# Weight groups of the KC chunk loaded between the stripes of x, the 112-column product moved into the VS chunk, and the last chunk finished per token tile

## What is computed

```python
u = RMSNorm(h)
[q | k/v x3 | nsa gates | z | xBC | dt | branch gates] = u @ W_in
A = NSA(q, ...)        # compressed + selected + sliding-window attention, a sigmoid gate per head
B = Mamba2-SSD(z, xBC, dt)
h = h + W_out( sigmoid(gA) * (A @ P_A) + sigmoid(gB) * (B @ P_B) )
h = h + relu(RMSNorm(h) @ W_up)^2 @ W_down
out = RMSNorm(h)
```

## Time and profile before

| | |
|---|---|
| median of 3 runs | 2117.24 us (2115.2 to 2118.54) |
| the profiled execution | 2118.04 us |
| its span, first to last instruction | 2116.4 us |
| mean granted clock of TensorE | 0.997 |
| TensorE busy | 2083.1 us, 98% of the span |
| VectorE busy | 1310.9 us, 62% |
| ScalarE busy | 977.1 us, 46% |
| GpSimd busy | 112.3 us, 5% |
| bytes moved | 383.59 MB, mean 181 GB/s |

### The profile page before, as it was taken

One profiled execution on the slowest core, in us unless ns is written; L12 is line 12 of the kernel. 1 busy time (PEld: TensorE's weight loads), 2 busy tenths in 40 slices (PEclk: granted clock), 3 DMA queues, 4 the chain that ended last, 5 costly groups with the idle time before them and its releaser, 6 DMA issues.

```text
span 2116.4 us, 28060 instructions
## 1 busy us (share of the span) xinstructions
PE 2083.1 (98%) x9760; PEld 1731.3 (82%) x9760; DVE 1310.9 (62%) x1780; ACT 977.1 (46%) x1323; POOL 112.3 (5%) x162
## 2 busy tenths in 40 slices
PE   7999999999999999999999999999999999999997
PEld 5788888888888888888888878888888888888886
DVE  5645666666665578886678865555555555555554
ACT  5434444444443455554455534444434434433443
POOL 3000000000000011111011100000000000000000
PEclk9999999999999999999999999999999999999999
DMA  8556464645466666665656556556566566666653
GB/s 234 186 166 188 140 179 139 177 138 174 138 197 195 175 179 188 181 184 195 188 170 183 183 197 207 179 183 189 190 195 184 188 194 184 188 195 193 184 191 133
DMA packets 196631, 383.59 MB, mean 181 GB/s; under 512 B 16192, under 2 KB 16288, under 8 KB 195120
## 3 DMA queue, kind: packets, MB, share of 16 engines
q1 hardware_dynamic: 193152, 365.87, 57.1%
q0 software_dynamic: 3344, 16.24, 2.2%
q10 hardware_dynamic: 32, 0.01, 0.0%
HBM read 379.91 MB, written 2.16 MB: 181 GB/s over the span
## 4 chain that ended last, share of the span: by engine, by line
PE 59%; issue 36%; DVE 2%; DMA 1%; ACT 1%; DVEq 0%; ACTq 0%; SPq 0%; POOLq 0%; POOL 0%
PE acc L284 17%; PE acc L286 17%; PE acc L285 17%; PE x L802 1%; PE tr L307 1%; DMA raw<-w_in 1%; PE x L738 1%; PE x L687 1%; PE tr L760 1%; DVE lo L251 1%; PE x L745 0%; PE tr L762 0%; PE tr L753 0%; PE tr L765 0%; PE x L814 0%
## 5 line engine op out<-in xcount | busy, mean ns | idle before, releaser
L251 DVE TENSOR_TENSOR lo<-raw,hi 128x1024 fp32r<-128x1024 f32 (+1 forms) x696 | 847.0, 1224 | 591.3 <-ACT hi L244 581.0
L244 ACT ACTIVATE hi<-raw 128x1024 fp32r<-128x1024 f32 (+1 forms) x696 | 724.5, 1052 | 699.6 <-PE acc L286 676.4
L284 PE MATMUL acc<-hi,LAh 128*128 128x512 f32 x1856 | 738.0, 398 | 4.0 <-DVE lo L251 4.0
L286 PE MATMUL acc<-hi,LAl 128*128 128x512 f32 x1856 | 724.1, 390 | 0.0
L285 PE MATMUL acc<-lo,LAh 128*128 128x512 f32 x1856 | 723.0, 390 | 0.0
L284 PEld LDWEIGHTS acc<-hi,LAh 128*128 128x128 f32 x1856 | 348.7, 188 | 78.0 <-issue 3.9
L286 PEld LDWEIGHTS acc<-hi,LAl 128*128 128x128 f32 x1856 | 348.4, 188 | 73.6
L285 PEld LDWEIGHTS acc<-lo,LAh 128*128 128x128 f32 x1856 | 348.8, 188 | 72.2 <-issue 1.7
L284 PE MATMUL acc<-hi,LBh 128*128 128x512 f32 x896 | 352.6, 394 | 2.7 <-DVE LBl L339 2.7
L286 PE MATMUL acc<-hi,LBl 128*128 128x512 f32 x896 | 350.0, 391 | 0.0
L285 PE MATMUL acc<-lo,LBh 128*128 128x512 f32 x896 | 349.8, 390 | 0.0
(11 more groups left out here) (267 smaller groups left out, 1174.1 us busy)
## 6 DMA issues: line engine op xcount, KB each, us to landing
raw<-w_in SPq DMA_DIRECT2D x304, 512.0 KB, 4.0
raw<-w_up SPq DMA_DIRECT2D x128, 512.0 KB, 3.9
raw<-w_down SPq DMA_DIRECT2D x128, 512.0 KB, 4.4
raw<-w_proj_ssm SPq DMA_DIRECT2D x64, 512.0 KB, 4.0
raw<-w_proj_nsa SPq DMA_DIRECT2D x32, 512.0 KB, 4.4
raw<-w_out SPq DMA_DIRECT2D x32, 512.0 KB, 4.4
W<-acs_rows POOLq DMA_DIRECT2D x8, 1024.0 KB, 5.0
GA<-x SPq DMA_DIRECT2D x4, 512.0 KB, 5.9
```

The lines of the kernel that those rows point to most:

```text
L244: act.activation(hi[:, sl, :, 0:n], raw[:, sl, :, 0:n], ACT.Copy).then_inc(s_hi, 1)
L251: dve.tensor_tensor(lo[:, sl, :, 0:n], raw[:, sl, :, 0:n], hi[:, sl, :, 0:n].bitcast(F32), ALU.subtract).then_inc(s_lo, 1)
L284: pe.matmul(o, xh, wh, start=(k == 0), stop=False)
L286: x = pe.matmul(o, xl, wh, start=False, stop=(k == KT - 1))
```

## The change

- The chunk `C_SMALL` is gone; every later chunk has a number lower by one. Its weights are loaded by GpSimd in two transfers (48 and 64 columns, all 2048 rows) once the first `compress` is done, split by ScalarE and VectorE in one piece each (`small_hi`, `small_lo`), and multiplied in four parts after groups 3 to 6 of the VS chunk. `gates_dt`, `softplus` and `cumsums` move to the KW chunk, the last turn and copies to the VW chunk.
- SP issues the weight groups of the KC chunk between the stripes of x. TensorE multiplies group 0 after two of the four stripes; the turns of the other two are hooks after groups 0 and 3.
- `angles` and `reduce_angles` move to slots 3 and 4 of the VC chunk, `sines` to slot 5, `columns` to slot 1. The squares of x move to slots 3 and 4 of the KC chunk.
- The counts of `s_lo` for the quarters of `w1` become 8n + 2q + 4.
- ScalarE runs a one-column copy before it needs its table for x.
- At the end TensorE does groups 6 and 7 of the last chunk first for token tile 0 and then for tile 1; adding, weighing, squares, variance and inverse root run per tile; the four stores wait for a piece each, and the last is issued by ScalarE.

```diff
-            for n in range(4):
+            def load_x(n):
                 sp.dma_start(GA[:, :, NC * n:NC * (n + 1)], x_rows[:, :, NC * n:NC * (n + 1)]).then_inc(s_x[n], 16)
+            load_x(0)
+            load_group(sp, C_KC, 0, w_in, 0, KC0)
+            load_group(sp, C_KC, 1, w_in, 0, KC0)
+            load_x(1)
+            load_group(sp, C_KC, 2, w_in, 0, KC0)
+            load_x(2)
+            load_group(sp, C_KC, 3, w_in, 0, KC0)
+            load_group(sp, C_KC, 4, w_in, 0, KC0)
+            load_x(3)
+            for j in (5, 6, 7):
+                load_group(sp, C_KC, j, w_in, 0, KC0)
-            load_chunk(sp, C_SMALL, w_in, 0, 0, extra=[(w_in, NG0, 0, 3 * NH), (w_in, DT0, 3 * NH, SH)])
...
-                    pool.wait_ge(s_lo, 8 * n + 2 * q + 6)
+                    pool.wait_ge(s_lo, 8 * n + 2 * q + 4)
...
+            pool.wait_ge(s_hid, 1)
+            pool.dma_start(SMG, w_in[:, :, NG0:NG0 + 3 * NH]).then_inc(s_smw, 16)
+            pool.dma_start(SMD, w_in[:, :, DT0:DT0 + SH]).then_inc(s_smw, 16)
...
+            turn_x(0)
+            turn_x(1)
+            mm_chunk(pe, C_KC, 0, LAh, LAl, {0: [lambda: turn_x(2)], 3: [lambda: turn_x(3)]},
+                     need={0: [(s_trd, 1)], 2: [(s_trd, 2)], 4: [(s_trd, 3)], 6: [(s_trd, 4)]})
+            mm_chunk(pe, C_VC, 1, LAh, LAl, {0: [turn_columns], 2: [lambda: pe_turn(pe, E_KC, XR, [(s_acc, C_KC + 1)])],
+                                             6: [lambda: compress(0)]})
+            mm_chunk(pe, C_KS, 0, LAh, LAl, {0: [compress_k2],
...
+            mm_chunk(pe, C_VS, 1, LAh, LAl, {0: [compress_v2],
+                                             2: [lambda: pe_turn(pe, E_KS, Y, [(s_rope, 1)])],
+                                             3: [lambda: small(0)], 4: [lambda: small(1)], 5: [lambda: small(2)],
+                                             6: [lambda: small(3)]})
+            mm_chunk(pe, C_KW, 0, LAh, LAl, {0: [turn_small], 6: [cumsum]})
...
+            slots(act, split_hi, C_KC, 8, {2: [lambda: split_x(3)], 3: [lambda: squares_of_x(0)], 4: [lambda: squares_of_x(1)],
+                                           7: [take_kc]})
+            slots(act, split_hi, C_VC, 8, {2: [lambda: copy_t(E_KC, KV[:, 0:2, :])], 5: [sines], 6: [lambda: hidden(0, 1)],
+                                           7: [lambda: take(C_VC, 1, XR[:, 0, :])]})
...
+            slots(dve, split_lo, C_KC, 8, {2: [lambda: split_x(3)], 7: [take_kc]})
+            slots(dve, split_lo, C_VC, 8, {1: [columns], 2: [lambda: blocks(0, E_KC, CPK)], 3: [angles, lambda: reduce_angles(0)],
+                                           4: [lambda: reduce_angles(1)], 6: [lambda: hidden(0)],
+                                           7: [lambda: take(C_VC, 1, XR[:, 1, :], C_VC + 1)]})
...
+            for t, done, v in ((0, s_l0, 1), (1, s_mm, 8 * C_END)):
+                dve.wait_ge(done, v)
+                dve.tensor_tensor(H[:, t, c3], acc[(C_END - 1) % 2][t][:, :], H[:, t, c3], ALU.add).then_inc(s_la, 1)
+                dve.drain()
+                dve.tensor_tensor(GB[:, t, c3], H[:, t, c3], GA[:, 0, c3], ALU.mult).then_inc(s_hw, 1)
+                last_variance(t)
+            for t, n in ((0, 1), (1, 0)):
+                dve.wait_ge(s_fr, t + 1)
+                dve.tensor_scalar(GB[:, t, HALF[n]], GB[:, t, HALF[n]], RS[:, t:t + 1], None, ALU.mult).then_inc(s_fin[t][n], 1)
```

More of the change, by code:

```diff
@@ L72 @@
 C_MLP = C_WO + 4
+C_END = C_MLP + 32
 C_END = C_MLP + 32
@@ L287, in mm_group, with mm_rows @@
             x.then_inc(s_mm, 1)
+        def mm_rows(pe, g, par, j, t, Lh, Ll):
+            sl = g % RING
+            pe.wait_ge(s_lo, g + 1)
+            for kk in range(2):
+                k = 2 * j + kk
+                o, xh, xl = acc[par][t][:, :], Lh[:, k, t * P:(t + 1) * P], Ll[:, k, t * P:(t + 1) * P]
+                pe.matmul(o, xh, hi[:, sl, kk, :], start=False, stop=False)
+                pe.matmul(o, xh, lo[:, sl, kk, :], start=False, stop=False)
+                x = pe.matmul(o, xl, hi[:, sl, kk, :], start=False, stop=(k == KT - 1))
+            return x
         def pe_event(pe, e, ready=()):
@@ L940, in hidden @@
                 act.activation(HT[:, :], X7[:, 0:NG * NCMP], ACT.Tanh, scale=0.5).then_inc(s_hta, 1)
-            slots(act, split_hi, C_SMALL, 8, {0: [lambda: squares_of_x(0)], 1: [lambda: squares_of_x(1)], 7: [copy_small]})
-            slots(act, split_hi, C_KC, 8, {1: [gates_dt], 2: [softplus], 6: [sines], 7: [lambda: take(C_KC, 1, XR[:, 0, :])]})
-            slots(act, split_hi, C_VC, 8, {0: [decay_ends, copy_cumsums], 2: [lambda: copy_t(E_KC, KV[:, 0:2, :])], 6: [lambda: hidden(0, 1)],
-                                           7: [lambda: take(C_VC, 0, XR[:, 0, :])]})
@@ new lines, in _ @@
+            slots(act, split_hi, C_VS, 8, {0: [small_hi], 2: [lambda: copy_t(E_KS, key_cols(0, 0))],
+                                           7: [lambda: take(C_VS, 1, V_(0, 0)), copy_small]})
+            slots(act, split_hi, C_KW, 8, {1: [gates_dt], 2: [softplus], 7: [lambda: take(C_KW, 0, XR[:, 0, :])]})
+            slots(act, split_hi, C_VW, 8, {0: [decay_ends, copy_cumsums], 2: [lambda: copy_t(E_KW, key_cols(1, 0))],
+                                           7: [lambda: take(C_VW, 1, V_(0, 1))]})
@@ L1099, in mlp @@
                     hk[8 * k + 10] = [lambda k=k: act_split_t(act, e + k, LAh, 4 * k)]
-                    if last:
+                    if last and k < 3:
                         hk[8 * k + 39] = [lambda k=k: residual_squares(C + 4 + k, k)]
@@ L1276, in take_rope, with small_lo @@
                 rope()
-            slots(dve, split_lo, C_SMALL, 8, {})
-            slots(dve, split_lo, C_KC, 8, {1: [gates_dt], 2: [columns, angles], 3: [softplus],
-                                           4: [lambda: reduce_angles(0)], 5: [lambda: reduce_angles(1)], 6: [cumsums], 7: [lambda: take(C_KC, 1, XR[:, 1, :], C_KC + 1)]})
-            slots(dve, split_lo, C_VC, 8, {2: [lambda: blocks(0, E_KC, CPK)], 6: [lambda: hidden(0)],
-                                           7: [lambda: take(C_VC, 0, XR[:, 1, :], C_VC + 1)]})
+            def small_lo():
+                for n, (c0, c1, src) in enumerate(((0, 3 * NH, SMG), (3 * NH, SMALL, SMD))):
+                    dve.wait_ge(s_smh, n + 1)
+                    dve.tensor_tensor(LBl[:, :, c0:c1], src, LBh[:, :, c0:c1].bitcast(F32), ALU.subtract).then_inc(s_sml, 1)
@@ L1290, in _ @@
+            slots(dve, split_lo, C_VS, 8, {1: [value_copy, small_lo], 2: [lambda: copy_t(E_KS, key_cols(0, 2))],
+                                           7: [lambda: take(C_VS, 1, V_(1, 0), C_VS + 1)]})
+            slots(dve, split_lo, C_KW, 8, {1: [gates_dt], 3: [softplus], 6: [cumsums], 7: [lambda: take_rope(C_KW, 0, C_KW + 1)]})
             slots(dve, split_lo, C_VW, 8, {2: [lambda: copy_t(E_KW, key_cols(1, 2))],
-                                           7: [lambda: take(C_VW, 0, V_(1, 1), C_VW + 1)]})
+                                           7: [lambda: take(C_VW, 1, V_(1, 1), C_VW + 1)]})
```

208 lines of the change are left out of this document (119 added, 89 removed).

## The result

The changed kernel takes 2102.7 us (median of 4 runs, 2102.09 to 2104.44) against 2116.22 us of the kernel before (4 runs, 2114.36 to 2118.54). The ratio is 0.9938, with a 95% interval of 0.9926 to 0.995. Run again later beside other kernels it took 2102.72 us against 2115.95. Two executions far from all others, 11179 us of the kernel before and 3535 us of the kernel of experiment 2, are left out of the ratios. The forecast was 2106.5 with a range of 2102.5 to 2110.5: the time lies inside, 0.2 us from its lower edge, and the gain is 13.5 us where 10.5 were summed. The profiled execution of the change took 2104.44 us, its span is 2102.8 us.

A forecast was written before the change was run, and what follows sets the result against it. TensorE, busy 98% of the span, was taken to bound the kernel, leaving its idle and slow time to win. Start -10.5, `w2` wait +1.9 and end -1.9 made -10.5 us; forecast 2106.5 us, range 2102.5 to 2110.5.

The forecast's parts named there:

- Start of group 0 at 12.0: KC chunk: TensorE free for group 0 at 12.0 us, after stripe 1 lands at 10.0 and is turned; bounds 11.6 to 13.0.
- The work that must be done from there, 34.9 us: From group 0's start to the point formerly at 59.0 us: TensorE's work without the listed waits takes 34.9 us.
- Slow pace, 1.6 us, bounds 0.9 and 2.7: First group of KC: TensorE's matmuls run at half pace at first, costing 1.6 us, bounds 0.9 and 2.7.
- No waits for splits in KC: KC chunk: ScalarE and VectorE keep ahead with the splits by margins of 1 to 2 us, each step covered.
- The rival that had them: KC chunk: late loads make groups 1 to 3 and 6 wait 1 to 1.5 us each, +4.5 us, 2111; chance 0.14.
- Wait for `w2`, 1.9 us, bounds 0 and 3: At `compress_k2`: TensorE waits 1.9 us for the `w2` loads, issued later by GpSimd; bounds 0 and 3.
- the rival that rested on a quick landing: At `compress_k2`: `w2` lands within about 4 us of issue, no wait, 1.9 us better, 2104.8; chance 0.20.
- The product of 112 columns, its weights and the chain behind it at nothing: VS and KW chunks: the moved product, its weight loads and `gates_dt`, `softplus`, `cumsums` are covered and cost nothing.
- The end, 1.9 us: After the last product: per-tile work lets the first store go out at 2.85 us, winning 1.9 us; bounds 1.0 and 2.2.
- The sum: Whole kernel: start -10.5, wait for `w2` +1.9, end -1.9, together -10.5 us; all bounds together -13.8 to -6.4.
- The slower rival: KC chunk: the slow pace lasts through it, eight groups costing 21.8 us instead of 1.6, 2126.7; chance 0.04.
- given back further on: KS or VS: short rows hold up the weights by 7 us or more, leaving 2113 to 2118; chance 0.05.

The follow-up runs named there:

- experiment 2: The kernel before with only the new end (`mm_last`, the chain per token tile, the four stores) and the old start: 2114.0 us, ratio 0.9991 to the kernel before.
- kernels without filling: Kernels with the new start and no unread transposes of the identity keeping TensorE busy before group 0; the changed kernel, 2102.7 us, is one.
- experiment 4: The changed kernel plus unread transposes of the identity, 5 before the turn of stripe 0 and 11 before that of stripe 1: 2101.45 us.
- experiment 6: The changed kernel with `angles` and both `reduce_angles` back in slots 4 and 5 of the KC chunk: 2103.88 us.
- experiment 3: The changed kernel with both `w2` loads issued ahead of the row norm on GpSimd, without a wait before them: 2099.99 us.
- Experiment 7: The changed kernel with ScalarE scaling its half of tile 0 right after that tile's squares and SP storing it first: 2102.09 us.

## Why the prediction was nearly right, step by step

- *What bounds the kernel*: right. The middle stayed as it was but for the pace behind the wait near 1230 us and small differences that cancel, and both gains lie in the first 60 us and behind the last product.
- *Start of group 0 at 12.0*: 11.75; right. Stripe 1 was turned at 10.13 where 10.0 was forecast, so the 1.65 us apiece for the stripes and groups held.
- *The work that must be done from there, 34.9 us*: this term was mis-sized, and it is the largest part of the error. The point that was at 59.01 comes at 59.01 - 10.2 (the mark's gain) - 1.3 (the new wait, which lies behind it) = 47.5, if all else up to the mark is as it was. Less 11.75 and 2.1 for the pace that is 33.7 us. (The wait also hid 0.15 us of a matmul's tail; with it the term is that much smaller.) I had taken 34.7 from the time between 13.5 and 59.0 less the listed waits, and corrected only for the tail that a wait hides. TensorE's timeline of the kernel before shows, around one of its waits, what more a wait costs:

```profile
39.94 0.39 PE L286 MATMUL acc<-hi,LAl 128*128 128x512 f32 x1
41.45 0.50 PE L284 MATMUL acc<-hi,LAh 128*128 128x512 f32 x1 [1.12 <-DVE lo L251]
41.79 0.39 PE L285 MATMUL acc<-lo,LAh 128*128 128x512 f32 x1
```

From the last matmul of the group to the next start are 1.51 us, not 0.23: the listed idle time of 1.12 and 0.16 of tail, as I had it. But the matmul after that starts 0.34 us later, not 0.23: 0.11 more that no list counts. Rows of the two kernels place most of the 1.2 us. The 112-column product is the same 48 matmuls in both. In the kernel before:

```profile
13.50 0.56 PE L654 MATMUL acc<-LAh,hi 128*112 128x256 f32 x1
...
14.07 0.29 PE L656 MATMUL acc<-LAh,lo 128*112 128x256 f32 x1
...
25.34 0.50 PE L284 MATMUL acc<-hi,LAh 128*128 128x512 f32 x1 [1.09 <-DVE lo L251]
```

and one of its four parts in the changed kernel:

```profile
113.24 0.28 PE L687 MATMUL x<-LAh,LBh 128*112 128x256 f32 x1
...
114.65 0.40 PE L291 MATMUL acc<-hi,LAh 128*128 128x512 f32 x1
```

Before, it took 11.84 us with 4.94 of four listed waits and 0.64 of their tails, so 6.26. In the changed kernel nothing interrupts a part, and four of 1.41 make 5.6. Of the 0.6 between, 0.3 is slow pace: the first two steps took 0.57 us where two take 0.24 later. It was in the 34.7 already, and I added the slow pace of the new start as a term of its own. The other 0.3 is 0.06 to 0.09 behind each of the three waits inside it. The six waits after them cost up to 0.11 apiece in the same way, together about 0.5. So about 1.1 of the 1.2 us has a place in these rows; the rest I can't place, and no experiment measured the term by itself.
- *Slow pace, 1.6 us, bounds 0.9 and 2.7*: 2.1 in the profiled run. Over the kernels without filling it was 2 to 12 slow matmuls at 0.2 us each, 0.4 to 2.4 us, so the lower bound was too high. In the old start it can last longer: experiment 2's profile has it until 6.9 us after a wait of 2.6. That idleness ahead is what costs it was right; experiment 4 shows it. The Trainium skill, "TensorE: Matmul & The Clock Gate", Part 1, says that the moment of the rise varies from run to run of the same program; the ten and seven slow matmuls in the two profiles of the changed kernel, with the rise near 16.2 and 14.8 us, agree.
- *No waits for splits in KC*: right, none. The rival that had them did not happen; experiment 6 shows how near it was: two tables in this chunk bring three such waits.
- *Wait for `w2`, 1.9 us, bounds 0 and 3*: right in place and cause (experiment 3), 1.3 us in size. The second issue stood 4.2 us ahead of TensorE's asking (66.75 against 70.92), as counted; it landed 5.4 us after it where I had 6.2. The Trainium skill, "DMA: Bandwidth & Descriptors", anatomy of one DMA, gives by its fit an estimate of 2.2 us for 64 KB; the landings here, beside other transfers, took 4.2 to 6.8, so the trace does not agree, and the rival that rested on a quick landing fell with it.
- *The product of 112 columns, its weights and the chain behind it at nothing*: right; the product ran from 113.2 to 127.1 us, where 105 to 130 was forecast, and no wait stands in the VS, KW and VW chunks.
- *The end, 1.9 us*: 2.1 in the profile. From the first store to the end of the span are 6.9 us in both kernels, so that the four stores run as one stream fits. Experiment 7 shows that the end follows the start of the first, though not in full: it went out 1.1 us after the last product instead of 2.6, and the span ended 8.4 us after it instead of 9.5, 1.1 of the 1.5.
- *The sum*: 10.5 was forecast. Measured term by term: 0.25 from the start of group 0, 1.2 from the work term and 0.6 from `w2` came out better, 0.5 from the pace worse, and 0.2 from the end better, so 12.3 us in the profiled pair (10.2 + 2.1). The pair differs by 1.3 more behind the mark, which no term of the sum held; nearly all of it is the chance length of a slow stretch. The medians say 13.5 and 13.2, with an interval of 2.5 us about them on either side; how much of their last us is such luck is left open. That the time fell inside the range, by 0.2 us, is luck too with such an interval; the mechanism, the places and the signs of the terms are what the runs bear out.
- *The slower rival*, the slow pace through KC, did not happen: it ended with group 0 at the latest in every kernel with the new start. Nor was the gain given back further on: behind the wait for `w2` no wait of TensorE for the `lo` of a weight group is in the list.

## What to carry to other kernels

When a kernel is at its engine's limit in the middle, its start and its end are what can be won: load in the order in which the first product needs its operands, and work that only needs to be done some time goes into a stretch where the lead is full. A wait costs its idle time, the tail it hides and the slower first products after it, here 0.16 and up to 0.11 us on top of 1.12, and the slow pace where it was long; add these before you sum. Moving a load's trigger in a chain of queues moves everything behind it on that queue: look for the last small load there, which is what was waited for here.
